# Router logits from the transposed residual rows, a shorter ladder of stages per token tile, and zero fills at other steps, in a two-layer diffusion-transformer step

## What is computed

```python
def residual_tail(x, heads_out, g1, sh2, sc2, g2, norm2_l, w_out_l, w_rg_l, w_re_l, w_gate_l, w_up_l, w_down_l):
    x = x + g1 * jnp.einsum('bte,ed->btd', heads_out, w_out_l)
    h2 = rmsnorm(x, norm2_l) * (1 + sc2) + sh2
    return x + g2 * hier_moe(h2, w_rg_l, w_re_l, w_gate_l, w_up_l, w_down_l)

def hier_moe(h, w_rg_l, w_re_l, w_gate_l, w_up_l, w_down_l):
    grp_logits = jnp.einsum('btd,dg->btg', h, w_rg_l).astype(jnp.float32)
    ...
    exp_logits = jnp.einsum('btd,de->bte', h, w_re_l).astype(jnp.float32).reshape(b, t, N_GROUPS, EXPERTS_PER_GROUP)
    ...
    top_val, top_idx = lax.top_k(exp_logits, TOP_K)
```

## Time and profile before

| | |
|---|---|
| median of 3 runs | 1493.14 us (1491.62 to 1494.76) |
| profiled execution, own time | 1492.42 us |
| its span in the profile | 1490.7 us |
| PE busy | 1243.9 us, 83% |
| DVE, ACT, POOL busy | 529.8, 378.9, 153.5 us |
| mean granted clock of PE | 0.908 of full speed |

### The profile page before, as it was taken

One profiled execution on the slowest core, in us unless ns is written; L12 is line 12 of the kernel. 1 busy time (PEld: TensorE's weight loads), 2 busy tenths in 40 slices (PEclk: granted clock), 3 DMA queues, 4 the chain that ended last, 5 costly groups with the idle time before them and its releaser, 6 DMA issues.

```text
span 1490.7 us, 16106 instructions
## 1 busy us (share of the span) xinstructions
PE 1243.9 (83%) x5588; PEld 700.5 (47%) x5588; DVE 529.8 (36%) x1349; ACT 378.9 (25%) x943; POOL 153.5 (10%) x251
## 2 busy tenths in 40 slices
PE   2999687849999868999929998799999885999970
PEld 0455354425655444544415555455565543444530
DVE  0131154425555251211132414544655443111116
ACT  0121154414443111111111214554443210111111
POOL 2210120000000020000022103000000011000005
PEclk9999878977999968999969997999999995999995
DMA  9976945692001457999973116630201158799945
GB/s 352 388 269 232 375 170 196 247 344 92 29 29 38 159 208 277 371 365 365 373 271 104 57 53 240 226 115 1 92 29 35 58 202 313 266 364 370 366 190 211
DMA packets 125209, 314.72 MB, mean 211 GB/s; under 512 B 9376, under 2 KB 57792, under 8 KB 112464
## 3 DMA queue, kind: packets, MB, share of 16 engines
q1 hardware_dynamic: 69408, 219.52, 39.9%
q10 hardware_dynamic: 43520, 53.48, 10.3%
q0 software_dynamic: 12208, 40.78, 7.3%
HBM read 233.04 MB, written 80.71 MB: 210 GB/s over the span
## 4 chain that ended last, share of the span: by engine, by line
PE 74%; DMA 7%; DVE 6%; issue 4%; ACTq 3%; SPq 2%; ACT 2%; POOL 1%; POOLq 0%; DVEq 0%
PE ps L624 16%; PE ps L697 15%; PE ps L560 10%; PE ps L432 8%; PE ps L717 7%; PE ps L469 7%; DMA ring<-in_w_mod 4%; PE ps L490 4%; PE ps L446 3%; ACTq L1074 2%; PE ps L647 1%; SPq L783 1%; SPq L803 1%; DMA arena<-in_w_mod 1%; PE ps L566 1%
## 5 line engine op out<-in xcount | busy, mean ns | idle before, releaser
L624 PE MATMUL ps<-ring,big 128*128 128x384 f32 (+2 forms) x640 | 233.3, 524 | 7.5 <-ACT big L1067 7.5
L432 PE MATMUL ps<-consts,arena 128*128 128x128 f32 (+2 forms) x888 | 137.6, 288 | 53.4 <-DVE arena L1427 21.0
L469 PE MATMUL ps<-arena 64*128 64x128 f32 (+5 forms) x576 | 147.2, 464 | 35.0 <-DVEq L1485 15.7
L697 PE MATMUL ps<-ring,arena 128*128 128x512 f32 x384 | 172.8, 604 | 2.4 <-DVE arena L1751 2.4
L624 PEld LDWEIGHTS ps<-ring,big 128*128 128x128 f32 x640 | 121.6, 192 | 111.5 <-issue 65.2
L432 PEld LDWEIGHTS ps<-consts,arena 128*128 128x128 f32 (+2 forms) x888 | 112.1, 161 | 117.7 <-issue 73.2
L560 PE MATMUL ps<-ring,big 128*128 128x512 f32 x320 | 144.4, 604 | 5.8 <-ACT arena L1022 4.1
L469 PEld LDWEIGHTS ps<-arena 64*128 64x128 f32 (+1 forms) x576 | 84.5, 214 | 100.2 <-issue 75.3
L981 ACT ACTIVATE arena<-ps 128x384 f32<-128x384 f32 (+3 forms) x140 | 69.1, 493 | 242.5 <-PE ps L432 232.7
L697 PEld LDWEIGHTS ps<-ring,arena 128*128 128x128 f32 x384 | 72.7, 195 | 86.1 <-issue 86.1
L560 PEld LDWEIGHTS ps<-ring,big 128*128 128x128 f32 x320 | 59.7, 192 | 79.0 <-issue 70.1
(11 more groups left out here) (182 smaller groups left out, 1325.2 us busy)
## 6 DMA issues: line engine op xcount, KB each, us to landing
slots<-zeros ACTq DMA_DIRECT2D x16, 2560.0 KB, 19.2
ring<-in_w_mod SPq DMA_DIRECT2D x20, 2048.0 KB, 15.4
ring<-in_w_up SPq DMA_DIRECT2D x22, 1024.0 KB, 9.2
ring<-in_w_gate SPq DMA_DIRECT2D x22, 1024.0 KB, 6.8
arena<-slots SPq DMA_DIRECT2D x32, 512.0 KB, 5.6
arena<-in_w_down SPq DMA_DIRECT2D x16, 1024.0 KB, 11.8
slots<-arena POOLq DMA_DIRECT2D x32, 512.0 KB, 9.2
ring<-in_w_down SPq DMA_DIRECT2D x14, 1024.0 KB, 11.4
```

Of the source, the lines that this page charges most:

```text
L432: return pe.transpose(out, in_, ident)
L469: mm = pe.matmul(two(2 * h)[:, at:at + hi - lo], queries(pr, h), keys(pr, h, lo, hi), start=(at % 512 == 0), stop=True, skip_group_check=True)
L624: mm = pe.matmul(ps[:, c, 0:CHUNKS[c][1]], hT[:, s, k, :], slot[c][:, k, 0:CHUNKS[c][1]], start=(k == 0), stop=(k == KD - 1))
L697: mm = pe.matmul(ps[:, b, :], xgT[:, b, k * P:(k + 1) * P], w_gu[q][:, :, k, :], start=(k == 0), stop=(k == KD - 1))
```

## The change

The router's product no longer takes the normalised row. PE transposes the residual row itself (stage TURN, from `heads`), the evictions multiply with the norm weight and (1 + scale) as a per-partition factor (`modc2`), and the row's norm factor and the part that comes from the shift (`bwr`, one product per kind of token and layer, `shift_logits`) are applied to the 24 logits by the first operation of `pick`. The two modulation columns that this needs are transposed in phase 2 (`mod_columns2`). The stages become OUT 0, TURN 2, NORM 3, ROUTE 4, POS 5; both halves of the norm stand in NORM. The route product goes to bank 6 (lane O) and is issued at the head of the next step (`ranks`). Of the 16 zero fills the first eight stay where they were, and the last eight stand at steps 0 to 3 of layer 0's phase 4, two behind each step's exponentials. The scatter of a tile now also waits for its normalised row, and POOL alternates norm factors and scatters.

```diff
@@ -57,7 +57,7 @@
 
 PROJ = [4 * i + 8 for i in range(TILES)]
 DEEP = 4
-OUT, NORM, H2, ROUTE, POS = 0, 4, 7, 10, 11
+OUT, TURN, NORM, ROUTE, POS = 0, 2, 3, 4, 5
 ORDER = [4, 0, 1, 2, 3]
 AT = [ORDER.index(t) for t in range(TILES)]
 MOD_AT = (5, 11, 18)
...
@@ -456,6 +460,24 @@
                     mm = transpose(ps[:, 7, c * P:(c + 1) * P], mrow[:, 0, c * P:(c + 1) * P])
                 mm.then_inc(M.full, 1)
 
+            def mod_columns2(L, g):
+
+                M.take(pe, ("mc2", L, g))
+                pe.wait_ge(mods_done, 3 * L + g + 1)
+                for c in range(4):
+                    mm = transpose(ps[:, 7, c * P:(c + 1) * P], mrow[:, g, c * P:(c + 1) * P])
+                mm.then_inc(M.full, 1)
+
+            def shift_logits(L):
+
+                M.take(pe, ("bw", L))
+                pe.wait_ge(mc2_done, 2 * (L + 1))
+                for kind in range(2):
+                    for k in range(KD):
+                        mm = pe.matmul(ps[:, 7, kind * RW:(kind + 1) * RW], modc2[:, kind, 0, k:k + 1].broadcast_to([P, P]),
+                                       wr[:, k, :], start=(k == 0), stop=(k == KD - 1), skip_group_check=True)
+                mm.then_inc(M.full, 1)
+
             def attention(L, phase):
                 pairs = PAIRS[phase]
@@ -516,14 +538,26 @@
                             if s in (at, at + 1) and (g < 2 or L < DEPTH - 1):
                                 ks = range(4 * (s - at), 4 * (s - at) + 4)
                                 mod_group(L + g // 2, (g + 1) % 3, ks)
+                        for g in (1, 2):
+                            if s == MOD_AT[g - 1] + 3:
+                                mod_columns2(L, g)
                         if s == MOD_AT[2] + 3 and L < DEPTH - 1:
                             mod_columns(L + 1)
                     if phase == 4:
+                        if s == 1:
+                            shift_logits(L)
                         beside(L, s)
 
             def ranks(L, s):
 
                 for i in range(TILES):
+                    if s - PROJ[i] == ROUTE:
+                        O.take(pe, ("rt", L, i))
+                        pe.wait_ge(M.free, M.freed[("h2", L, i, 1)])
+                        for k in range(KD):
+                            mm = pe.matmul(ps[:, 6, 0:RW], h2T[:, k * P:(k + 1) * P], wr[:, k, :],
+                                           start=(k == 0), stop=(k == KD - 1))
+                        mm.then_inc(O.full, 1)
                     if s - PROJ[i] == POS:
                         O.take(pe, ("pos", L, i))
                         pe.wait_ge(pick_done, TILES * L + i + 1)
@@ -540,13 +574,13 @@
 
                 for i in range(TILES):
                     t, n = ORDER[i], s - PROJ[i]
-                    if n in (H2, H2 + 1):
-                        half = n - H2
+                    if n in (TURN, TURN + 1):
+                        half = n - TURN
                         M.take(pe, ("h2", L, i, half))
-                        pe.wait_ge(h_done, h2_no(L, i))
+                        pe.wait_ge(res_done, 2 * (TILES * L + i) + half + 1)
                         for k in range(4):
                             mm = transpose(ps[:, 7, k * P:(k + 1) * P],
-                                           h2_rows(i)[:, (4 * half + k) * P:(4 * half + k + 1) * P])
+                                           heads[:, i, (4 * half + k) * P:(4 * half + k + 1) * P])
                         mm.then_inc(M.full, 1)
                     if n in (OUT, OUT + 1):
                         half = n - OUT
@@ -560,13 +594,6 @@
                             mm = pe.matmul(ps[:, 7, :], hoT[:, i, k, :], slot[2 + half][:, k, :],
                                            start=(k == 0), stop=(k == KD - 1))
                         mm.then_inc(M.full, 1)
-                    if n == ROUTE:
-                        M.take(pe, ("rt", L, i))
-                        for k in range(KD):
-                            mm = pe.matmul(ps[:, 7, 0:RW], h2T[:, k * P:(k + 1) * P], wr[:, k, :],
-                                           start=(k == 0), stop=(k == KD - 1))
-                        mm.then_inc(M.full, 1)
-
             def turn_entry(L, i):
 
                 T.take(pe, ("h", L, i), frees=2)
@@ -804,6 +831,7 @@
                 if half == 0:
                     sp.dma_start(consts[:, :], t_in["consts"]).then_inc(const_in, 16)
                     sp.dma_start(n1c[:, :, :], t_in["norm1"]).then_inc(n1_in, 16)
+                    sp.dma_start(n2c[:, :, :], t_in["norm2c"]).then_inc(n2_in, 16)
                     x_load(t_in["x0"], 0)
             in_load(0, 0)
             x_load(t_in["x0"], 1)
@@ -1002,6 +1030,8 @@
                                 exps(s, h)
                     if 4 <= s < len(pairs) + 4:
                         outputs(s - 4)
+                    if phase == 4 and L == 0 and s < 4:
+                        zero_fill(2 * s + 8, 2 * s + 10)
                     if phase == 4 and s == len(pairs) + 2:
                         first_weights(L)
                     if phase == 4:
@@ -1016,11 +1046,16 @@
             def beside(L, s):
                 for i in range(TILES):
                     n = s - PROJ[i]
-                    if n in (H2, H2 + 1):
-                        half = n - H2
-                        act.wait_ge(M.full, M[("h2", L, i, half)])
-                        act.activation(h2T[:, half * 512:(half + 1) * 512], ps[:, 7, :],
-                                       ACT.Copy).then_inc(M.free, 1)
+                    if n == TURN:
+                        kind = int(ORDER[i] == 4)
+                        act.wait_ge(M.full, M[("h2", L, i, 0)])
+                        act.wait_ge(mc2_done, 2 * (L + 1))
+                        if i:
+                            act.wait_ge(O.full, O[("rt", L, i - 1)])
+                        for k in range(4):
+                            cp = act.activation(h2T[:, k * P:(k + 1) * P], ps[:, 7, k * P:(k + 1) * P], ACT.Copy,
+                                                scale=modc2[:, kind, 1, k:k + 1])
+                        cp.then_inc(M.free, 1)
                     if n in (OUT + 2, OUT + 3):
 
                         half = n - OUT - 2
@@ -1083,7 +1118,8 @@
                 for s in range(TILES + 1):
                     if L == 0:
 
-                        zero_fill(2 * s, 2 * s + 2)
+                        if s < 4:
+                            zero_fill(2 * s, 2 * s + 2)
                     if s < TILES:
                         i = s
                         kv = 5 if ORDER[i] == 4 else ORDER[i]
@@ -1131,8 +1167,6 @@
                 attention(L, 2)
                 meet(act, "act")
 
-                if L == 0:
-                    zero_fill(12, NE)
                 for i in range(TILES + 1):
                     if i < TILES:
                         act.wait_ge(T.full, T[("uq", L, i)])
@@ -1327,21 +1361,18 @@
                 def scatter(i):
 
                     t = ORDER[i]
+                    pool.wait_ge(h_done, h2_no(L, i))
                     pool.wait_ge(idx_done, TILES * L + i + 1)
                     for j in range(2):
                         at = j * TILES + t
                         pool.indirect_dma_start(slots, bass.IndirectOffsetOnAxis(ap=sidx[:, at:at + 1], axis=0),
                                                 h2_rows(i), None).then_inc(scat_out, 16)
 
-                entry2(0)
-                entry2(1)
-                entry2(2)
-                if L == 0:
-                    pool.wait_ge(zero_out, 16 * NE)
                 for i in range(TILES):
+                    entry2(i)
+                    if L == 0 and i == 0:
+                        pool.wait_ge(zero_out, 16 * NE)
                     scatter(i)
-                    if i + 3 < TILES:
-                        entry2(i + 3)
 
                 E0 = NE * L
                 if L < DEPTH - 1:
@@ -1398,6 +1429,29 @@
                 STT(modc[:, :, 1, :], modc[:, :, 1, :], 1.0, n1c[:, L:L + 1, :].broadcast_to([P, 2, KD]), ALU.add,
                     ALU.mult).then_inc(mc_done, 1)
 
+            def mod_columns2(L, g):
...
+                then(dve, "dve", TT(bwr[:, :, :], ps[:, 7, 0:2 * RW].rearrange("p (a b) -> p a b", a=2),
+                                    cst["pad"].unsqueeze(1).broadcast_to([P, 2, RW]), ALU.add))
+                dve.sem_inc(M.free, 1)
+
             def blend(L, i, a, b):
 
                 dve.wait_ge(y_in[i], 32 * (L + 1))
@@ -1508,6 +1562,8 @@
 
                 for s in range(STEPS[phase] + 1):
                     turning = 3 <= s < len(pairs) + 3
+                    if phase == 4 and s == 2:
+                        shift_logits(L)
                     if phase == 4 and s >= 1:
                         projected(L, s - 1)
                     for h in range(2):
@@ -1536,6 +1595,10 @@
                         dve.wait_ge(M.full, M[("out", L, i, half)])
```

(11 more changed lines are left out.)

27 lines of the change are left out of this document (25 added, 2 removed).

## The result

| | before | after |
|---|---|---|
| median of the runs | 1493.95 us | 1527.37 us (4 runs, 1526.73 to 1536.25) |
| ratio to before, 95% interval | | 1.0239, 1.0199 to 1.0279 |
| profiled execution, span | 1490.7 us | 1525.1 us |

The change makes the kernel 2.4% slower (2.2% by the two medians; one of the four runs after, 1536.25, lies 8 us above the others). The forecast was 1517.8 us with a range of 1500 to 1533; the side is right, and 9 us of slowing were not in the sum (profiled execution: 1526.73).

What follows compares the result with a forecast made beforehand. PE was taken as three quarters of the chain, so waits count only there. 12.5 (fills) + 4.3 and 2.4 (ladders) + 5.0 (shift_logits) + 0.7 (columns) + 0.5 (norm load) = 25.4 us on 1492.4: 1517.8, range 1500 to 1533.

Steps and rivals of the forecast that it cites:

- The fills: Layer 0: 44.6 us added in phase 4, 20.1 behind phase 2 and 12.0 in the projection removed; net +12.5 us.
- pairs that drain: Rival: fill pairs in phase 4 drain between steps at 4.1 us each, so the kernel takes 1487 us; chance 0.07.
- issues nearly free: Rival: each fill issue costs only 0.55 us, so the kernel takes 1478 us; chance 0.03.
- Pick inside attention and step 21: Phase 4: picks at steps 13 and 17 add 4.6 us a layer; tile i = 3's second half starts 5.2 us later.
- The tail: Last tile's projection to last scatter, second half at 7.1 us: scatter starts 0.3 us earlier in layer 0, 2.2 in layer 1.
- ladder, layer 0: Phase 4 tile stages of layer 0: +4.6 inside attention and -0.3 at the end, together +4.3 us.
- columns, stage C: mod_columns2, four transposes twice a layer: only layer 1's second set is uncovered, +0.7 us.
- shift_logits, stage D: New products ahead of step 2's scores in layer 1: 3.4 to 6.7 us, taken as +5.0; hidden under the fills in layer 0.
- ladder, layer 1: Phase 4 tile stages of layer 1: +4.6 inside attention and -2.2 at the end, together +2.4 us.
- the ladder gives more: Rival: the gate step does not in effect wait for the pick, 13.2 us less, 1505 us; chance 0.13.
- The norm weights' load: SP's new load ahead of the first weights: +0.5 us, between 0 and 1.1.
- Half clock for the second half: Rival: the last tile's second half takes 14.3 us at half clock, +7.1 a layer, 1532 us; chance 0.11.

Runs made afterwards that it cites:

- b_fills_moved: Kernel before with only the zero fills moved as in the change; 1506.94 us against 1490.69, ratio 1.0118.
- b_fills_sync: Kernel before with ten fills on ACT in the projection and the last six issued by SP in one train in layer 0's phase 4; 1459.54 us against 1489.68.
- c_gate_sync_late_w: c_gate_sync with SP's last two loads of expert weights moved behind the loads of the scattered rows; 1458.20 us, ratio 0.9794.
- c_gate_first: Changed kernel with DVE's gate step in its own loop ahead of the pick; 1508.73 us, ratio 1.0122.
- c_fills_back: Changed kernel with the zero fills where the kernel before had them; 1516.76 us, ratio 1.0175.
- c_gate_sync: c_gate_first with the last six fills issued by SP as in b_fills_sync; 1457.62 us, ratio 0.9798.
- b_fills_apart: b_fills_sync with SP's six fills spread two, two, one and one behind the first four residual half rows; 1455.60 us, ratio 0.9777.
- c_early_shift: c_gate_sync with shift_logits moved from step 1 of phase 4 to step 10 of phase 2; 1455.48 us, ratio 0.9767.

## Why the prediction was right, and where it was short

**The fills (12.5): right.** The pieces came as written: uq 12.6 us earlier (12.0 in the sum), from there to the first output projection 23.7 us longer (24.5), eight issues of 55.2 us in all instead of 51.8. The net was 11.1 with layer 0's new products under it, and 9.0 and 8.4 in the profiles in which the fills alone were moved; the timed runs of b_fills_moved say 12.5 to 22.7. The mechanism, a blocked queue with waiters behind it, is shown by b_fills_sync. Both fast rivals (pairs that drain, issues nearly free) fell with the seven rows of 6.6 to 11.8 us. By the Trainium skill ("DMA: Bandwidth & Descriptors", section "Issuing engines are not separate DMA queues") the issues would be small beside the transfers; for fills of this size in a row the trace does not agree: seven of the eight issues took 6.6 to 11.8 us.

**Pick inside attention and step 21 (4.6, then 5.2): right.** From the first output projection to step 20 it was +5.3 in both layers. The second half of tile i = 3 stood 17.2 us behind the first, where I had 15.8: I took turn and values at full clock (0.8 and 1.24), and they took 1.33 and 2.40 behind the 4.19 us wait.

**The tail (-0.3, and -2.2 in layer 1): the step that failed.** I wrote "second half 7.1" and left the slow second half to a rival at 14.3. It took 10.16 us in layer 0 and 8.60 in layer 1, between the two. The last scatter, for which I took before's duration, took 6.07 and 7.09 us. That it shared the DMA engines with expert weights is shown by c_gate_sync_late_w.

The sum by its own stages, as the profiled execution has them (8.9 us over the forecast in all):

| term | forecast | measured | off |
|---|---|---|---|
| fills and the norm load, stage A | +13.0 | +11.1 | -1.9 |
| ladder, layer 0 | +4.3 | +9.4 | +5.1: the slow half 3.1, the scatter 1.8 |
| columns, stage C | +0.7 | +1.4 | +0.7 |
| shift_logits, stage D | +5.0 | +5.9 | +0.9 |
| ladder, layer 1 | +2.4 | +8.7 | +6.3: steps 20 to 24 2.3, step 24 to the last scatter 2.8, the rest in the steps ahead and in the scatter with the load behind it |
| experts of layer 1 to the end | 0 | -2.1 | -2.1 |

The total hides how far the ladders were off: forecast at 6.7 us for both, measured at 18.1. That it still came within the range is in part luck, since stages A and F were 4 us below the sum; why F got shorter I have no run to say.

In layer 1 I had let the last tile's first half run at full clock and the turn behind it come sooner, as before's trace has it. The changed kernel does neither: its first half takes 8.83 us there too. That fast half was no lasting property of before's layer 1 either: in b_fills_moved, with the same instructions there, it took 8.83.

**What lies behind the failed step.** That the gate step stands behind the pick was in my sum as 0.85 us of "hand-over" at each pick, with PE's wait at about 2.9 to 4 us. I priced the wait by its own length. c_gate_first shows its whole price, some 10 us a layer. And the rival "the ladder gives more" named what would lift it, that the gate step doesn't wait for the pick; I gave it 3.3 us for each of two steps and a layer, and only 0.13, since the pick can't start earlier. It was DVE's order, not the pick's start, that could be changed.

**shift_logits (5.0, hidden in layer 0): right.** Stage D grew by 5.9; with the fills taken away, layer 0 shows 3 us of it (c_fills_back, c_gate_sync), so it was hidden by them.

**The norm weights' load (0.5):** the second group of modulation products starts at 33.54 us, where it started at 33.75. No cost is seen.

**Half clock for the second half (the slower rival):** the mechanism was there, at 10.16 and 8.60 us instead of 14.3. The clock came back within the half, as the window from 555 to 560 shows (0.93).

## What to carry to other kernels

The idea of the change was sound and its placing was not: with the fills on a queue that nobody waits for, the gate step ahead of the pick, the new products under a wait for weights, and the pick split behind the one operation that frees a shared bank, the same change is 3.7% faster than the kernel before instead of 2.4% slower. Of these 3.7%, 2.2% are the fills alone, which the kernel before can have as well (b_fills_apart, 1455.60 on the same chip); the shorter ladder, well placed, is worth the other 21.6 us. When stages are drawn together, write down for each in-order engine which of its inputs is ready first: here DVE took a long chain of small operations that waited for a route ahead of one operation whose input had been ready for 2 us, and PE waited for the latter. And price an idle wait of PE with the slower work behind it: 4.19 us of waiting ahead of a half projection were followed by 3 us more for that half in layer 0 and 1.5 in layer 1.

## What I had not expected of the hardware

- The stretch at the 1.2 GHz level at the start of phase 4 isn't the same for the same instructions: stage D of layer 1 took 63.1 us in some kernels and 67.5 in others (c_gate_first, c_gate_sync_late_w), with nothing changed in it. A difference of 4 to 5 us between two single profiles of this kernel can be that alone. What sets its length stays open.
- Products of 24 columns with a new 128x128 tile each keep the weight loads busy all the time: `shift_logits` takes 3.75 us for 32 at full clock (c_early_shift; PEld is busy for 3.50 of 3.50 us in it) and 5.9 to 6.9 where the clock is falling. I have no run with fewer loads, so that they are the bound is read from this alone.
- Six fills issued back to back by SP blocked it for 39.17 us, where the six behind the second blocked ACT for 42.85 us; so the block is not ACT's alone. The second issue of a train takes longer than those behind it, 9.09 us before and 11.76 after; I have no run that says why.
